# Feed-forward parts of a two-block transformer kernel: the first modulation pair leaves the weight ring for idle context columns

## The chip, the cores and the metric

The kernel runs on one core of one Trainium2 chip. The time is that of the device, in microseconds, from a launch with one program; three runs of the kernel before took 2731.29, 2735.66 and 2738.76 us. Five engines work side by side and wait for each other by semaphores: TensorE (PE in the profile, its weight loads PEld), VectorE (DVE), ScalarE (ACT), GpSimd (POOL) and SyncE (SP), which here only issues the DMA transfers.

## The reference, cut to what matters

Two blocks of different design are computed one after the other, all in float32, for 512 tokens of width 1024 and a context of 256 tokens.

```python
def first_block(x, ...):
    for layer in range(2):
        h = rmsnorm(x, norm_mix_g[layer])
        if layer == 0:                       # Fourier heads and convolution heads
            y = concat(fnet_heads(p[..., :512], ...), conformer_conv_heads(...)) @ w_out_ab
        else:                                # windowed means
            y = pool_mixer(h, pool_map, pool_scale)
        x = x + y
        h = rmsnorm(x, norm_ffn_g[layer])
        x = x + (silu(h @ w_gate[layer]) * (h @ w_up[layer])) @ w_down[layer]
    return rmsnorm(x, final_g)

def second_block(x, c, ctx, c_ctx, ...):
    for i in range(2):
        mod_x = silu(c) @ w_ada[i] + b_ada[i]          # six modulation vectors
        mod_c = silu(c_ctx) @ w_ada[i] + b_ada[i]
        ...                                            # attention over x and ctx (layer 0: window, 1: differential)
        x = layer_norm(alpha * x + g1 * ax, ln1_g[i], ln1_b[i])
        x = layer_norm(alpha * x + g2 * sqrelu_mlp(x * (1 + sc2) + sh2, ...), ln2_g[i], ln2_b[i])
        ...                                            # layer 0 only: the same for ctx
```

The modulation vectors depend on `c` alone, so the kernel computes those of layer f of the second block inside feed-forward part f of the first one: the weights `w_ada` are cut into pairs of blocks, and pair after pair is worked off beside the products of gate, up and down.

## The kernel before, in words

**Data.** Activations lie with the features on the partitions: `X`, `Ahi`, `Alo` are [128, 8, 768], eight tiles of features by 512 token columns and 256 context columns. A float32 product is made of three products of high and low parts (weight high x activation high, weight high x activation low, weight low x activation high), so every weight and every activation is split in two. In the whole first block only the token columns of `Ahi` and `Alo` are written or read; the context columns are first used by the norm n5 ahead of the attention.

**The weight stream.** All large weights are one list of blocks of 1 MB, `stream`, laid out by the host in the order of use. Block b goes to slot b % 3 of a ring (`RING = 3`, tiles `raw`, `whi`, `wlo`), in two halves. SP waits until PE has used the same half of block b - 3 (`freed`, by the counter `w_used`) and issues the load (L452). POOL splits each half: L526 writes `whi`, L528 writes `wlo` (semaphore `w_split`). Modulation blocks are not split: PE multiplies them from `raw` (`ada`, L868), or DVE sums them up (L1966, L1970). `SPLITS[b]` counts the splits ahead of block b, and `is_ada` says which blocks have none.

**Order on PE.** `columns` (L685) multiplies one block, or two in turns, tile k by tile k: for each k first gate's share, then up's (L675 by way of `product`). It waits for the split of the first half at k = 0 and of the second at k = 4, and, where a norm goes before, for the k-th tile of `Alo` (semaphore `ready`).

**A feed-forward part** (`swiglu`, one on each engine). Its 57 blocks in the ring begin with modulation pair 0 (two blocks), gate 0, up 0; then eleven steps follow, each with gate and up of the next step, a modulation pair and down of this step. PE first multiplies pair 0 (L868), then gate 0 and up 0 in turns. For the first part these are blocks 10 and 11 (pair), 12 (gate), 13 (up); in the second 68 to 71. So up 0 takes the slot of the pair's first block and its load waits for PE to have used that. Block 9, the last of the output projection, doesn't use the ring; it is loaded to the arena once the four Fourier heads are done.

**Later parts and the order on POOL.** POOL's work is one hand-written list: `split_run(first, end)` splits blocks, as a loop over whole rounds of the ring where there are two or more, and between these runs stand other jobs. One is `norm_residual` (L627 to L640): X times the norm's scale for eight tiles (L636; L634 for l2), then gain and bias for eight tiles (L639). It follows the layernorms l1, l2 and l3, waits for DVE's copy of the scale (`kept`; L1813, L1811), and makes the residual into which DVE adds an MLP's results. The places where the list is cut are given by `ring_end(b)` (L563), the next multiple of 3 at or above b:

```python
split_run(ring_end(B_WOA), ring_end(B_ML0 + 2))     # L643
norm_residual("l1", 1, X_CTX)
split_run(ring_end(B_ML0 + 2), ring_end(B_QKV + 2))
norm_residual("l2", 2, X_ONLY)
...
split_run(B_WOB, ring_end(B_ML1 + 2))               # L663
norm_residual("l3", 3, X_ONLY)
```

The block numbers before: pooling 67, keys and values 125, queries 127, window attention's output 131, first MLP (`B_ML0`) 135, differential attention's weights (`B_QKV`; query, key, value for each of four steps) 167, its output 179, second MLP (`B_ML1`) 183, 215 blocks in all.

**An MLP** (`mlp`): PE does up(0), then for each step up(i + 1) and down(i). Block +0 is up 0, +1 is up 1, +2 is down 0, +3 is up 2. A down product is eight tiles m; tile m waits until DVE has added the tile `slots` places earlier to X (`dfree`), with two slots where the context goes along (first MLP) and four without it (second). DVE's first addition (L2224) waits for the whole residual, `dve.wait_ge(l1_res or l3_res, 8)` at L2233.

**Differential attention**: PE does the query products, the key products (`key_products`), waits for both halves of the value block's split (L1217), does two tiles of value products (L1210) and then the first scores (L1233).

## Time and profile before

| | us |
|---|---|
| runs | 2731.29, 2735.66, 2738.76 (median 2735.66) |
| the profiled execution | 2737.59 |
| its span, first to last instruction | 2735.3 |
| PE busy | 2595.5 (95%) |
| DVE busy | 1478.3 (54%) |
| POOL busy | 1357.7 (50%) |
| ACT busy | 649.8 (24%) |
| mean granted TensorE clock | 0.978 |

PE is busy nearly all the time. Busy shares say little about a single wait, though: for that one reads a stretch of the timeline, in which each row has the start, the time, the engine, the line and the form of an instruction, and in brackets how long the engine sat idle before it and who released it. "PE ... [6.20 <-POOL wlo L528]" means that PE waited 6.20 us for POOL's write of `wlo`. The granted clock is a share of full speed, 1.00 for 2.4 GHz and 0.50 for 1.2 GHz. Where several equal instructions are merged, the row has their number (x8) and the time of all.

### The profile page before, as it was taken

Reading aid. Unit: us, or ns where it says so; the run is one execution under the profiler, and the core shown is the slowest. Engines: PE = TensorE matmul, PEld = TensorE weight load, DVE = VectorE, ACT = ScalarE, POOL = GpSimd, SP = SyncE. Lnnn points to the kernel's source line nnn. Section 1 sums busy time; section 2 is a strip of 40 time slices with the busy share of each in tenths; the row PEclk is TensorE's granted clock in tenths of the full one; section 3 lists DMA queues with packets and bytes.
Section 4 is the critical chain, followed back from the end, with each engine's and each line's share of the span. In section 5 each row is a group of like instructions: output and inputs, shape, how many; then the busy total and the mean of one; then the engine's idle time right before and its main releaser. Section 6 shows DMA issues by size and latency. Waiting matters only on the chain.

```text
span 2735.3 us, 39085 instructions
## 1 busy us (share of the span) xinstructions
PE 2595.5 (95%) x14176; PEld 2101.6 (77%) x14176; DVE 1478.3 (54%) x2473; ACT 649.8 (24%) x1220; POOL 1357.7 (50%) x880
## 2 busy tenths in 40 slices
PE   7989999999999989889989999999899999899997
PEld 6668777777777768656768888888688887688886
DVE  6955666456666645455454333333676665454445
ACT  2220000031000013477231111111265552211112
POOL 6374566645555663233536444444252515776661
PEclk9999999999999999899999999999999999999998
DMA  5124444434444441100111111221111011232321
GB/s 189 54 78 139 151 154 149 151 118 146 151 153 154 153 133 62 32 1 1 39 39 62 62 61 61 66 65 61 39 47 46 31 47 48 73 96 92 97 94 54
DMA packets 67388, 235.73 MB, mean 86 GB/s; under 512 B 8144, under 2 KB 9552, under 8 KB 67152
## 3 DMA queue, kind: packets, MB, share of 16 engines
q1 hardware_dynamic: 65792, 233.64, 26.5%
q8 instruction: 63, 1.03, 0.2%
q10 hardware_dynamic: 1488, 0.69, 0.1%
q14 instruction: 45, 0.37, 0.0%
HBM read 232.21 MB, written 2.10 MB: 86 GB/s over the span
## 4 chain that ended last, share of the span: by engine, by line
PE 87%; DVE 7%; ACT 2%; issue 2%; POOL 1%; DMA 1%; SPq 0%; DVEq 0%; ACTq 0%; POOLq 0%
PE ps L675 70%; PE ps L1210 2%; PE ps L1233 2%; PE ps L830 2%; PE ps L1098 2%; PE ps L1172 2%; PE ps L1084 1%; PE ps L794 1%; DVE X L1796 1%; PE ps L1164 1%; DVE Alo L1785 1%; DVE tmp L1778 1%; DMA raw<-in_stream 1%; PE ps L1059 1%; PE ps L718 1%
## 5 line engine op out<-in xcount | busy, mean ns | idle before, releaser
L526 POOL TENSOR_SCALAR whi<-raw 128x1024 fp32r<-128x1024 f32 x332 | 372.8, 1123 | 1019.5 <-DMA raw<-in_stream 1019.2
L528 POOL TENSOR_TENSOR wlo<-raw,whi 128x1024 fp32r<-128x1024 f32 x332 | 804.2, 2422 | 27.7
L675 PE MATMUL ps<-Ahi,whi 128*128 128x512 f32 (+1 forms) x2128 | 728.2, 373 | 40.4 <-DVE Alo L1785 18.8
L675 PE MATMUL ps<-Alo,whi 128*128 128x512 f32 (+1 forms) x2128 | 721.8, 370 | 0.0
L675 PE MATMUL ps<-Ahi,wlo 128*128 128x512 f32 (+1 forms) x2128 | 719.2, 369 | 0.0
L2224 DVE SCALAR_TENSOR_TENSOR X<-ps,modT,X 128x512 f32<-128x512 f32 (+1 forms) x384 | 242.4, 659 | 476.7 <-PE ps L675 476.5
L675 PEld LDWEIGHTS ps<-Ahi,whi 128*128 128x128 f32 x2128 | 375.7, 190 | 120.6 <-DVE Alo L1785 18.9
L675 PEld LDWEIGHTS ps<-Ahi,wlo 128*128 128x128 f32 x2128 | 376.2, 190 | 69.6
L675 PEld LDWEIGHTS ps<-Alo,whi 128*128 128x128 f32 x2128 | 376.7, 191 | 66.7 <-issue 0.7
L675 PE MATMUL ps<-hhi,whi 128*128 128x512 f32 x1120 | 373.6, 370 | 2.1 <-DVE X L2224 1.1
L675 PE MATMUL ps<-hhi,wlo 128*128 128x512 f32 x1120 | 373.4, 370 | 0.0
L675 PE MATMUL ps<-hlo,whi 128*128 128x512 f32 x1120 | 370.4, 368 | 0.0
L675 PEld LDWEIGHTS ps<-hhi,whi 128*128 128x128 f32 x1120 | 192.6, 188 | 45.5 <-issue 4.4
L675 PEld LDWEIGHTS ps<-hlo,whi 128*128 128x128 f32 x1120 | 192.3, 188 | 38.9
L675 PEld LDWEIGHTS ps<-hhi,wlo 128*128 128x128 f32 x1120 | 192.4, 188 | 38.5
L1326 ACT ACTIVATE hhi<-tmp 128x512 fp32r<-128x512 f32 (+1 forms) x108 | 73.7, 695 | 606.3 <-DVE tmp L2210 445.5
L1970 DVE SCALAR_TENSOR_TENSOR ps<-raw,arena,ps 128x256 f32<-128x256 f32 x432 | 174.0, 480 | 41.7 <-DMA raw<-in_stream 41.7
L1994 DVE TENSOR_TENSOR X<-ps,X 128x512 f32<-128x512 f32 x176 | 121.7, 692 | 137.3 <-PE ps L675 136.9
L1326 ACT ACTIVATE arena<-ps 128x256 f32<-128x256 f32 (+5 forms) x194 | 101.6, 543 | 245.4 <-PE ps L889 67.3
L625 POOL TENSOR_SCALAR tmp<-tmp,sm 128x256 f32<-128x256 f32 (+2 forms) x96 | 63.3, 662 | 148.1 <-DVE sm L2179 148.0
L1476 ACT ACTIVATE tmp<-ps 128x512 f32<-128x512 f32 x44 | 26.3, 598 | 425.0 <-PE ps L675 424.0
L1623 ACT ACTIVATE tmp<-ps 128x512 f32<-128x512 f32 x96 | 47.1, 525 | 293.1 <-PE ps L675 290.8
(300 smaller groups left out, 2851.0 us busy)
## 6 DMA issues: line engine op xcount, KB each, us to landing
raw<-in_stream SPq DMA_DIRECT2D x428, 512.0 KB, 3.8
X<-in_xT SPq DMA_DIRECT2D x2, 1024.0 KB, 6.6
arena<-in_dft SPq DMA_DIRECT2D x1, 2048.0 KB, 17.1
out_xT<-X SPq DMA_DIRECT2D x2, 1024.0 KB, 4.3
X<-in_ctxT SPq DMA_DIRECT2D x1, 1024.0 KB, 19.4
w<-in_stream SPq DMA_DIRECT2D x2, 512.0 KB, 4.3
vec<-in_vec SPq DMA_DIRECT2D x1, 364.5 KB, 7.7
arena<-in_fmap SPq DMA_DIRECT2D x1, 256.0 KB, 12.6
```

The costliest lines, as they stand in the source:

```text
L526: pool.tensor_scalar(whi[:, s, part], raw[:, s, part], 1.0, 1.0, ALU.mult, ALU.mult).then_inc(sem("w_hi"), 1)
L528: pool.tensor_tensor(wlo[:, s, part], raw[:, s, part], whi[:, s, part], ALU.subtract).then_inc(sem("w_split"), 1)
L625: pool.tensor_scalar(prob, prob, sm[:, u % 8, 2:3], 1.0, ALU.mult, ALU.mult).then_inc(sem("pA"), 1)
L675: mm = pe.matmul(dst[c], w[:, b % RING, off:off + P], rhs(k, part, c0, n), start=(k == 0 and w is whi and part == 0), stop=(k == kn - 1 an ...
L830: mm = pe.matmul(ps[:, WOUT_BANK[j], :], w[:, at:at + P], a[:, k, 0:T], start=(k == 0 and w is hi and a is Ahi), stop=(k == KT - 1 and w i ...
L1098: mm = pe.matmul(ps[DH * h:DH * h + DH, 6, 0:2 * P], vA[:, ks[t], DH * g:DH * g + DH], heads[:, h], start=(t == 0), stop=(t == len(ks) - 1 ...
L1172: mm = pe.matmul(ps[:, 6, :], vB[:, t, hh * P:(hh + 1) * P], aT[:, t, :], start=(t == 0), stop=(t == NTT - 1))
L1210: mm = pe.matmul(ps[:, 6 + t % 2, 0:256], a[:, k, t * P:(t + 1) * P], w[:, (B_QKV + 2) % RING, k * 256:(k + 1) * 256], start=(k == 0 and a ...
L1326: return act.activation(dst, src, ACT.Copy, scale=scale)
L1970: mm = dve.scalar_tensor_tensor(out=to, in0=row, scalar=c, in1=acc, op0=ALU.mult, op1=ALU.add)
L1994: dve.tensor_tensor(X[:, m, 0:T], ps[:, 4 + m % 2, :], X[:, m, 0:T], ALU.add).then_inc(sem(f"{name}_dfree"), 1)
L2224: mm = dve.scalar_tensor_tensor(out=X[:, m, c0:c0 + n], in0=ps[:, 4 + len(cols) * (m % (4 // len(cols))) + c, 0:n], scalar=mod(l, 5, m, c) ...
```

## The change

The first modulation pair of each feed-forward part is taken out of the ring. Its two blocks go straight to the context columns of `Ahi` and of `Alo`, which lie unused in the first block (`first_pair`, `load_first_pair`); PE multiplies them from there (`ada_first`), at the same place as before. The stream in memory stays as it was; the ring skips two blocks of it for each part, so that a part has 55 blocks in the ring, the ring's block numbers after the second part are lower by 4, and loads add 2 or 4 to find a block in memory. Gate 0 and up 0 are now the first blocks of a part in the ring (10 and 11; 66 and 67). Their halves are split in turns: gate's first, up's first, gate's second, up's second (`split_pair`); the same is done for the first two blocks of the input projection and of the window attention's output projection, and PE's waits in `columns` follow that order. The list of POOL is otherwise written as before, with the new block numbers in it: pooling 65, keys and values 121, queries 123, window attention's output 127, `B_ML0` 131, `B_QKV` 163, its output 175, `B_ML1` 179, and 211 blocks in the ring.

The diff, without the hunks that only change block offsets in DVE's and ACT's steps:

```diff
--- before.py
+++ after.py
@@ -111,7 +111,7 @@
 
 B_WIN = 0
 B_WOUT = B_WIN + 6
-FF_BLOCKS = 5 * FF_IT + 2
+FF_BLOCKS = 5 * FF_IT
 B_FF = [B_WOUT + 4, B_WOUT + 4 + FF_BLOCKS + 1]
 B_POOL = B_FF[0] + FF_BLOCKS
 B_KV = B_FF[1] + FF_BLOCKS
@@ -122,7 +122,8 @@
 B_QKV = B_ML0 + ML_BLOCKS
 B_WOB = B_QKV + 12
 B_ML1 = B_WOB + 4
-N_BLOCKS = B_ML1 + ML_BLOCKS
+RING_BLOCKS = B_ML1 + ML_BLOCKS
+N_BLOCKS = RING_BLOCKS + 4
 B_ML = [B_ML0, B_ML1]
 
 
@@ -131,17 +132,17 @@
     for first in B_FF:
         at = b - first
         if 0 <= at < FF_BLOCKS:
-            if at < 4:
-                return at < 2
+            if at < 2:
+                return False
             if at >= FF_BLOCKS - 3:
                 return at < FF_BLOCKS - 1
-            return (at - 4) % 5 in (1, 3)
+            return (at - 2) % 5 in (1, 3)
     return False
 
 
 
 SPLITS = [0]
-for _b in range(N_BLOCKS):
+for _b in range(RING_BLOCKS):
     SPLITS.append(SPLITS[-1] + (0 if is_ada(_b) else 2))
 FF_SPLITS = 18
 ADA_GROUP = 32
@@ -247,6 +248,10 @@
         Ahi = sb("Ahi", [P, KT, TT], F32R)
         Ahi_at = nc.sbuf_base - 4 * KT * TT
         Alo = sb("Alo", [P, KT, TT], F32R)
+        Alo_at = nc.sbuf_base - 4 * KT * TT
+
+        first_pair = [nc.alloc_sbuf_tensor_at(f"pair{e}", [P, KT, TT], F32, offset=at)[:, :, T:TT]
+                      for e, at in enumerate((Ahi_at, Alo_at))]
 
         whi = sb("whi", [P, RING, BLK], F32R)
         raw = sb("raw", [P, RING, BLK])
@@ -469,6 +474,14 @@
                 for half in range(2):
                     sp.wait_ge(*when("w_used", 2 * (b - RING) + half + 1))
                     load(b, b % RING, half)
+            def load_first_pair(f):
+
+                if f:
+                    sp.wait_ge(*when("pair_used", 2))
+                for e in range(2):
+                    sp.dma_start(first_pair[e], ins["stream"][B_FF[f] + 2 * f + e].rearrange("p (k c) -> p k c", k=KT)).then_inc(sem(f"pair{e}"), 16)
+
+            load_first_pair(0)
             sp.wait_ge(*when("y_done", HEADS_A))
             for half in range(2):
                 part = slice(half * HALF, (half + 1) * HALF)
@@ -477,37 +490,42 @@
             def freed(b, half, rounds=0):
                 sp.wait_ge(*when("w_used", 2 * RING * rounds + (2 * (b - RING) + half + 1)))
 
-            def load_run(first, end):
+            def load_run(first, end, skipped):
+
                 for b in range(first, end):
                     for half in range(2):
                         freed(b, half)
-                        load(b, b % RING, half)
+                        load(b + skipped, b % RING, half)
 
             def load_swiglu(f):
                 B0 = B_FF[f]
+                S = B0 + 2 * f + 4
+                load_run(B0, B0 + 2, 2 * f + 2)
                 with sp.Fori(0, FF_IT // 3) as p:
-                    for b in range(B0 + 4, B0 + 19):
-                        at = (b - B0 - 4) // 5 * 5 + B0 + 4 + FF_ORDER[(b - B0 - 4) % 5]
+                    for n in range(15):
+                        at = n // 5 * 5 + S + FF_ORDER[n % 5]
                         for half in range(2):
-                            freed(b, half, 5 * p)
-                            load(15 * p + at, b % RING, half)
-                for b in range(B0 + 49, B0 + 54):
+                            freed(B0 + 2 + n, half, 5 * p)
+                            load(15 * p + at, (B0 + 2 + n) % RING, half)
+                for n in range(45, 53):
+                    at = S + (45 + FF_ORDER[n - 45] if n < 50 else n)
                     for half in range(2):
-                        freed(b, half)
-                        load(B0 + 49 + FF_ORDER[b - B0 - 49], b % RING, half)
-
-            load_run(last + 1, B_FF[0] + 4)
+                        freed(B0 + 2 + n, half)
+                        load(at, (B0 + 2 + n) % RING, half)
+
+            assert last + 1 == B_FF[0]
             load_swiglu(0)
-            load_run(B_FF[0] + 54, B_FF[1] + 4)
+            load_run(B_POOL, B_POOL + 1, 2)
+            load_first_pair(1)
             load_swiglu(1)
-            first, rounds = -(-(B_FF[1] + 54) // RING), N_BLOCKS // RING
-            load_run(B_FF[1] + 54, first * RING)
+            first, rounds = -(-B_KV // RING), RING_BLOCKS // RING
+            load_run(B_KV, first * RING, 4)
             with sp.Fori(first, rounds) as i:
                 for s in range(RING):
                     for half in range(2):
                         freed(s, half, i)
-                        load(RING * i + s, s, half)
-            load_run(rounds * RING, N_BLOCKS)
+                        load(RING * i + (s + 4), s, half)
+            load_run(rounds * RING, RING_BLOCKS, 4)
 
 
             for h in range(2):
@@ -531,6 +549,12 @@
 
                 for half in range(2):
                     split(b % RING, half, 16 * rounds + (16 * (b // RING) + 16), more + (SPLITS[b] + half + 1))
+
+            def split_pair(b):
+
+                for half in range(2):
+                    for n in range(2):
+                        split((b + n) % RING, half, 16 * ((b + n) // RING) + 16, SPLITS[b] + 2 * half + n + 1)
 
             def split_run(first, end):
 
@@ -549,15 +573,14 @@
 
             def split_swiglu(f):
                 B0 = B_FF[f]
-                for b in (B0 + 2, B0 + 3):
-                    split_block(b)
+                split_pair(B0)
                 with pool.Fori(0, FF_IT // 3) as p:
                     for s in range(3):
                         for b in (0, 2, 4):
-                            split_block(B0 + 4 + 5 * s + b, FF_SPLITS * p, 5 * p)
+                            split_block(B0 + 2 + 5 * s + b, FF_SPLITS * p, 5 * p)
                 for i in range(FF_IT // 3 * 3, FF_IT - 1):
                     for b in (0, 2, 4):
-                        split_block(B0 + 4 + 5 * i + b)
+                        split_block(B0 + 2 + 5 * i + b)
                 split_block(B0 + FF_BLOCKS - 1)
 
             def ring_end(b):
@@ -606,7 +629,8 @@
                     pool.tensor_tensor(ending[:, side, :, e0:e0 + EDGE], own[:, :, e0:e0 + EDGE], edge[:, :, side, :],
                                        ALU.add).then_inc(sem("bands"), 1)
 
-            split_run(0, B_WOUT + 3)
+            split_pair(B_WIN)
+            split_run(2, B_WOUT + 3)
             for half in range(2):
                 b = B_WOUT + 3
                 part = slice(half * HALF, (half + 1) * HALF)
@@ -618,7 +642,8 @@
             split_swiglu(0)
             split_block(B_POOL)
             split_swiglu(1)
-            split_run(B_KV, ring_end(B_WOA))
+            split_run(B_KV, B_WOA)
+            split_pair(B_WOA)
             for u in range(N_UNITS):
                 pool.wait_ge(*when("denA", u + 1))
                 prob = probA[u % 4][:, 1:1 + len(keys(UNITS[u][2])) * P]
@@ -640,7 +665,7 @@
                                        ALU.add).then_inc(sem(f"{name}_res"), 1)
 
 
-            split_run(ring_end(B_WOA), ring_end(B_ML0 + 2))
+            split_run(B_WOA + 2, ring_end(B_ML0 + 2))
             norm_residual("l1", 1, X_CTX)
             split_run(ring_end(B_ML0 + 2), ring_end(B_QKV + 2))
             norm_residual("l2", 2, X_ONLY)
@@ -662,7 +687,7 @@
                     split_run(B_QKV + 11, B_WOB)
             split_run(B_WOB, ring_end(B_ML1 + 2))
             norm_residual("l3", 3, X_ONLY)
-            split_run(ring_end(B_ML1 + 2), N_BLOCKS)
+            split_run(ring_end(B_ML1 + 2), RING_BLOCKS)
 
 
         @block.tensor
@@ -691,7 +716,7 @@
                         pe.wait_ge(*when(ready, k + 1))
                     for n, (ws, at) in enumerate(blocks):
                         if k % 4 == 0:
-                            pe.wait_ge(*when("w_split", ws + (k // 4 + 1)))
+                            pe.wait_ge(*when("w_split", ws + (k // 4 + 1 if len(blocks) == 1 else k // 2 - n + 1)))
                         for j in range(2):
                             mm = product(dsts[2 * n + j], cols, at, k * 256 + j * P, a_rhs, k, KT)
                             if j == 0 and k == KT - 1:
@@ -871,6 +896,16 @@
                                        skip_group_check=True)
                     mm.then_inc(sem("w_used"), 1)
 
+            def ada_first(f, e):
+
+                pe.wait_ge(*when(f"pair{e}", 16 * f + 16))
+                for k in range(KT):
+                    g = k % 4
+                    mm = pe.matmul(ps[ADA_GROUP * g:ADA_GROUP * (g + 1), 6 + e, 0:256],
+                                   csil[:, k, 2 * (ADA_SHARED - 1):2 * (ADA_SHARED - 1) + ADA_GROUP], first_pair[e][:, k, :],
+                                   start=(k < 4), stop=(k >= 4), skip_group_check=True)
+                mm.then_inc(sem("pair_used"), 1)
+
             def ada_select(name, copies):
 
                 pe.wait_ge(*when(f"{name}_arow", copies))
@@ -928,13 +963,13 @@
                             ada_columns(name, copies)
 
                 for e in range(2):
-                    ada(B0 + e, e, 0, 1)
-                columns(f"{name}_up", [(SPLITS[b], b) for b in (B0 + 2, B0 + 3)], X_ONLY, banks[0:4], ready)
+                    ada_first(f, e)
+                columns(f"{name}_up", [(SPLITS[b], b) for b in (B0, B0 + 1)], X_ONLY, banks[0:4], ready)
                 ada_select(name, 2)
 
                 with pe.Fori(0, FF_IT // 3) as p:
                     for s in range(3):
-                        i, at = 3 * p + s, B0 + 4 + 5 * s
+                        i, at = 3 * p + s, B0 + 2 + 5 * s
                         for part in range(2):
                             up(i + 1, at, FF_SPLITS * p, part)
                             if s == 0 and part == 0:
...
@@ -1459,16 +1494,19 @@
             def swiglu(f, name):
                 B0 = B_FF[f]
 
-                def rows(b_a, gap):
+                def rows(b_a):
                     for e in range(2):
-                        act.wait_ge(*block_used(b_a + gap * e))
+                        if b_a is None:
+                            act.wait_ge(*when("pair_used", 2 * f + e + 1))
+                        else:
+                            act.wait_ge(*block_used(b_a + e))
                         copy(arow[:, e, :], ps[:, 6 + e, 0:256]).then_inc(sem(f"{name}_arow"), 1)
 
                 def step(i, b, slot, first, shared_rows=False):
 
                     for j in range(2):
                         if j:
-                            act.wait_ge(*block_used(b + 2 if first else b))
+                            act.wait_ge(*block_used(b))
                         else:
                             act.wait_ge(*when(f"{name}_up", 2 * i + 1))
                         if not first:
...
```

## Rows read from the trace of the kernel before

**Rows 1.** The page: the span and the busiest engine, and the chain by engine.

```profile
span 2735.3 us, 39085 instructions
...
PE 87%; DVE 7%; ACT 2%; issue 2%; POOL 1%; DMA 1%; SPq 0%; DVEq 0%; ACTq 0%; POOLq 0%
```

**Rows 2.** The page, DMA issues: count, KB each, median us from issue to landing.

```profile
raw<-in_stream SPq DMA_DIRECT2D x428, 512.0 KB, 3.8
```

**Rows 3.** Timeline of PE, 187 to 202: start, us, form, [idle before <-releaser].

```profile
190.01 0.50 PE L675 MATMUL ps<-Ahi,whi 128*128 128x512 f32 x1 [0.46 <-DVE Alo L1754]
...
197.87 0.80 PE L675 MATMUL ps<-Ahi,whi 128*128 128x512 f32 x1 [6.20 <-POOL wlo L528]
```

**Rows 4.** Timeline of POOL, 185 to 198.

```profile
185.90 1.05 POOL L526 TENSOR_SCALAR whi<-raw 128x1024 fp32r<-128x1024 f32 x1 [18.12 <-DMA raw<-in_stream]
...
195.16 2.66 POOL L528 TENSOR_TENSOR wlo<-raw,whi 128x1024 fp32r<-128x1024 f32 x1
```

**Rows 5.** Stretches of PE: us, busy (matmuls), granted clock, DMA share, GB/s.

```profile
197.80:201.90 4.10, 4.03 (x10) 0.50 0.02 5
...
205.00:215.00 10.00, 10.00 (x46) 1.00 0.17 52
...
622.90:628.60 5.70, 5.70 (x13) 0.50 0.34 104
```

**Rows 6.** Timeline of PE, 616 to 624.

```profile
622.90 0.79 PE L675 MATMUL ps<-Ahi,whi 128*128 128x512 f32 x1 [4.93 <-POOL wlo L528]
```

**Rows 7.** Timeline of DVE, 617 to 624.

```profile
617.99 0.68 DVE L1754 TENSOR_TENSOR Alo<-tmp,Ahi 128x512 fp32r<-128x512 f32 x1
...
620.56 0.73 DVE L1763 SCALAR_TENSOR_TENSOR tmp<-X,vec,ps 128x512 f32<-128x512 f32 x1
...
621.22 2.17 DVE L1754 TENSOR_TENSOR Alo<-tmp,Ahi 128x512 fp32r<-128x512 f32 x1
```

**Rows 8.** Timeline of PE, 19 to 29.

```profile
23.22 0.79 PE L675 MATMUL ps<-Ahi,whi 128*128 128x512 f32 x1 [0.74 <-POOL wlo L528]
```

**Rows 9.** Stretch, all engines: busy (x) of each, then granted clock, DMA share, GB/s.

```profile
105.00:130.00 25.00, 25.00 (x74) 10.93 (x72) 24.92 (x39) 6.76 (x10) 0.00 (x0) 1.00 0.00 1
```

**Rows 10.** Timeline of PE, 1428 to 1456.

```profile
1430.59 0.52 PE L675 MATMUL ps<-Ahi,wlo 128*128 128x512 f32 x2
...
1453.14 0.51 PE L675 MATMUL ps<-hhi,whi 128*128 128x512 f32 x2
```

**Rows 11.** Timeline of POOL, 1400 to 1450.

```profile
1424.80 17.34 POOL L636 TENSOR_TENSOR X<-X,rstd 128x768 f32<-128x768 f32 x8 [27.88 <-DVE rstd L1813]
1442.14 7.77 POOL L639 TENSOR_SCALAR X<-X,rg,rb 128x768 f32<-128x768 f32 x8
```

**Rows 12.** Line L636 of POOL, 1424 to 1432: min/median/max ns.

```profile
L636 POOL TENSOR_TENSOR X<-X,rstd x5: 1825/1837/2575, 1424.8 to 1432.0; 128x768 f32<-128x768 f32 x5
```

**Rows 13.** Timeline of DVE, 1445 to 1453.

```profile
1451.34 1.14 DVE L2224 SCALAR_TENSOR_TENSOR X<-ps,modT,X 128x512 f32<-128x512 f32 x2 [10.92 <-PE ps L675]
```

**Rows 14.** Timeline of PE, 2367 to 2386.

```profile
2368.75 0.49 PE L675 MATMUL ps<-Ahi,whi 128*128 128x512 f32 x1 [0.77 <-ACT tmp L1623]
...
2385.37 0.39 PE L675 MATMUL ps<-hhi,whi 128*128 128x512 f32 x1
```

**Rows 15.** Timeline of POOL, 2355 to 2381.

```profile
2363.27 11.83 POOL L636 TENSOR_TENSOR X<-X,rstd 128x512 f32<-128x512 f32 x8 [15.88 <-DVE rstd L1813]
2375.09 6.05 POOL L639 TENSOR_SCALAR X<-X,rg,rb 128x512 f32<-128x512 f32 x8
```

**Rows 16.** Timeline of DVE, 1986 to 1989.

```profile
1987.82 0.68 DVE L1811 COPY X<-ps 128x512 f32<-128x512 f32 x1
```

**Rows 17.** Timeline of POOL, 1985 to 2018.

```profile
1999.74 11.02 POOL L634 TENSOR_TENSOR X<-X 128x512 f32<-128x512 f32 x8
```

**Rows 18.** Timeline of PE, 2002 to 2014.

```profile
2004.61 0.28 PE L1210 MATMUL ps<-whi,Ahi 128*128 128x256 f32 x1
...
2013.01 1.30 PE L1233 MATMUL ps<-k,q 128*128 128x384 f32 x6 [2.48 <-DVE rstd_r L2284]
```

More of the change, by code:

```diff
@@ L944, in swiglu @@
                 i = FF_IT - 2
-                at = B0 + 4 + 5 * i
+                at = B0 + 2 + 5 * i
                 for part in range(2):
@@ L952, in swiglu @@
                 i = FF_IT - 1
-                b = B0 + 4 + 5 * i
+                b = B0 + 2 + 5 * i
                 for e in range(2):
@@ L1482, in step @@
                         copy(hhi[:, slot, j, 0:T], tmp[:, j, 0:T]).then_inc(sem(f"{name}_hi"), 1)
-                rows(B0, 1)
+                rows(None)
                 step(0, B0, 0, True)
@@ L1487, in swiglu @@
                     for s in range(3):
-                        step(3 * p + s + 1, 15 * p + (B0 + 4 + 5 * s), (s + 1) % 3, False, s == ADA_SHARED - 1)
-                step(FF_IT - 1, B0 + 4 + 5 * (FF_IT - 2), (FF_IT - 1) % 3, False)
-                rows(B0 + 4 + 5 * (FF_IT - 1), 1)
+                        step(3 * p + s + 1, 15 * p + (B0 + 2 + 5 * s), (s + 1) % 3, False, s == ADA_SHARED - 1)
+                step(FF_IT - 1, B0 + 2 + 5 * (FF_IT - 2), (FF_IT - 1) % 3, False)
+                rows(B0 + 2 + 5 * (FF_IT - 1))
             rms("n2", "wout_evac", 0)
@@ L2009, in swiglu @@
                 for j in range(2):
-                    hidden(0, B0 + 3, j, True)
+                    hidden(0, B0 + 1, j, True)
                 mods(0, 0, 1)
@@ L2016, in swiglu @@
                         for e in range(2):
-                            ada_sums(p, 3 * p + s, e, B0 + 5 + 5 * s + 2 * e, s or e)
+                            ada_sums(p, 3 * p + s, e, B0 + 3 + 5 * s + 2 * e, s or e)
                         if s == ADA_SHARED - 1:
                             dve.wait_ge(*when(f"{name}_acc", ADA_SUMS * ADA_SHARED * (p + 1)))
-                        step(3 * p + s, 15 * p + (B0 + 4 + 5 * s), (s + 1) % 3, p if s == ADA_SHARED - 1 else None)
-                step(FF_IT - 2, B0 + 4 + 5 * (FF_IT - 2), (FF_IT - 1) % 3, last=True)
+                        step(3 * p + s, 15 * p + (B0 + 2 + 5 * s), (s + 1) % 3, p if s == ADA_SHARED - 1 else None)
+                step(FF_IT - 2, B0 + 2 + 5 * (FF_IT - 2), (FF_IT - 1) % 3, last=True)
                 mods(4, 10, 2)
```

## The prediction

> **What bounds the kernel now.** I read the page's chain first: TensorE (PE) carries 87% of the path that ends last, and the span is 2735.3 us [rows 1]. So an edit is worth what it adds to or takes from PE's idle time, plus what that idle time costs in clock. Second, I looked in the timelines of PE for the gaps at the places the diff touches, and third, in those of POOL and DVE, for what stands behind each gap. POOL is the engine that splits each half block of weights into a high and a low part, and it runs a list in a fixed order; what the change does to that order matters as much as the waits it means to remove.
>
> **Part 1, the starts of the feed-forward parts: a gain.** At the first one PE does gate's share of k = 0 from 190.01 and then waits 6.20 us for the low part of up's first half [rows 3]. POOL begins the four halves of gate and up only at 185.90, when gate's first half lands behind the two modulation blocks, and finishes the third, up's first, at 195.16 + 2.66 = 197.8 [rows 4]. After the wait PE runs 4.1 us at a granted clock of 0.50, the lower level of 1.2 GHz, with some ten matmuls where the later stretch at 1.00 has 46 in 10 us [rows 5]; half of that time is lost: 2.05. At the second part the wait is 4.93 us [rows 6], followed by 5.7 us at 0.50 [rows 5], 2.85 lost. There up's block could not even be loaded before PE had used the modulation block in its slot. Together 6.2 + 2.05 + 4.93 + 2.85 = 16.0 us.
>
> With the pair outside the ring, gate and up of the first part wait for the two blocks of the output projection that the pair waited for, so gate is released two blocks, some 24 matmuls or 5.4 us, earlier: POOL starts by 180.5. At 1.50 + 2.70 a half under contention (the spacing that makes 185.90 to 197.8 out of three halves is 4.0), up's first half, now second in line, is done by 188.9, before PE's first product at 190.01 [rows 3]; gate's second half is done by 193.1 and up's by 197.3, and PE needs them after 48 matmuls, at about 200.5. What is late next is DVE's low part of the activations, whose steps take 0.73 + 0.68 = 1.4 us alone and 0.73 + 2.17 = 2.9 us where a split is in the way, every second one at most [rows 7], against 12 matmuls, 2.7 us, of PE work for each; I cost that at nothing. At the second part both blocks are released when the first part ends, some 30 us ahead: no wait is left.
>
> The pair's own loads (2 x 1 MB, in pieces of 1 KB) cost SP two issues. The first two stand ahead of SP's wait for the Fourier heads, in a stretch in which the DMA engines are idle, its later part at 0.00 [rows 9]; the second two stand behind the pooling block's load and ahead of gate's. The trace has no load of that shape: at nothing, since over 30 us cover it, or, if the pieces took three times the 3.8 us of a half block [rows 2] each half, 23 us more ahead of gate's load, still covered. PE's sixteen pair matmuls stay the same in number and place.
>
> Splitting earlier puts POOL beside DVE's closing additions and norm. DVE's subtraction of two SBUF operands takes 0.68 us alone and 2.17 us once POOL splits; its product that reads PSUM stays at 0.73 us in the same stretch [rows 7]. The subtractions were beside splits before as well, and what newly lies beside them (additions from PSUM, the scaled products) is of the second kind, so this is nothing. The Trainium skill, "SBUF — State Buffer", section "Who interferes with whom", says that a DVE instruction with two SBUF inputs contends with a GpSimd instruction that reads SBUF, and one with at most one does not: the trace agrees. Were every DVE instruction slowed, two on the chain to the first product would cost 3 us, and the sum would be 3 us higher.
>
> **Part 2, the first projection's halves in turns: a small gain.** PE waits 0.74 us for its second block's first half [rows 8]; in turns this half is second in POOL's list instead of third. PE is at the low clock around it, and a row without the pause may let the clock rise sooner: 0.7 to 2.5 us, 1.0 taken. The same turns at the attention's output projection: its splits are ready there already, nothing.
>
> **Part 3, the ring is four blocks shorter: losses that the diff doesn't show.** Every later block has a number lower by 4, and 4 is not a multiple of 3. `ring_end(b)` rounds up to a multiple of 3, and POOL's list is cut there: it splits up to `ring_end(...)`, then does `norm_residual`, then splits on.
>
> *l1.* Before, B_ML0 is 135 and the cut 138: POOL splits the MLP's blocks +0, +1, +2 and then does the residual. After, B_ML0 is 131 and the cut 135: +3 goes ahead of the residual as well, and its slot is that of +0, so its second half can be loaded only when PE has finished the MLP's first product, at 1431.1 [rows 10]. Plus 3.8 us of landing [rows 2] is 1434.9; plus 3.5 to 4.2 for the split, 1438.8. Before, the residual starts at 1424.80 and ends at 1449.9 [rows 11]. Its products take 1.84 us beside nothing [rows 12], so now 1438.8 + 8 x 1.84 + 7.77 = 1461.3. DVE may add down's results to X only after it; its first addition, 1.14 us for both column groups [rows 13], ends at 1462.4 instead of 1452.5. Down has two slots, so PE's third tile waits for it: it begins at 1453.14 now [rows 10], 9.3 us later then. PE idles this long, and comes back at the low clock [rows 5]: 2.4 more (the mean of 2.05 and 2.85). **11.7 us.**
>
> *l3.* B_ML1 goes from 183 to 179, the cut from +3 to +4: the same. The first product ends at 2368.75 - 0.77 = 2368.0 [rows 14]; landing 2371.8; split 2375.7. The residual took 11.83 + 6.05 [rows 15]; alone, by the width, 8 x 1.84 x 2/3 = 9.8, so 10.5 taken: 2392.2; one addition, 1.14 for 768 columns [rows 13] and so some 0.8 for 512: 2393.0. Here four slots stand, and PE's fifth tile begins at 2385.37 [rows 14]: 7.6 later, with the clock **10.0 us**.
>
> *l2.* B_QKV goes from 167 to 163, the cut from +4 back to +2: the residual comes ahead of the split of the value weights (+2). It can start when DVE's copy ends, 1988.5 [rows 16], and takes 11.02 + 6.05 (the second figure is that of the other residual of this width) [rows 15, 17]: 2005.6. Two halves at 3.5 to 4.2: 2013.0. PE begins the value products at 2004.61 today [rows 18], and they last until 2013.01 - 2.48 = 2010.5, 5.9 us: to 2018.9 then, and the scores follow at 2018.9 instead of 2013.01. 5.9, and with the clock **8.3 us**.
>
> **The sum.** Gains 16.0 + 1.0 = 17.0, losses 11.7 + 10.0 + 8.3 = 30.0: 13.0 us slower, 2748.3 against the profiled span. The profiled execution took 2737.6 with what lies around its span, the median of the runs is 2735.7, so I add the 13.0 to the median: 2748.7.
>
> **The rivals.**
> *Hidden residuals, faster.* The three residuals are later, but PE isn't held: DVE would find other work, or the blocks land sooner. Then only the gains are left, 2735.7 - 17.0 = 2718.7. It decides the other way from the point at which l1's residual ends before about 1451, ten us earlier than worked out. DVE's list has the addition next, and nothing in the trace lets it pass; the rows speak against it.
> *No clock cost.* The pauses of 6 to 9 us don't bring the clock down, or PE's work behind them has slack. For it: DVE has room to catch up. Against: both pauses before [rows 5]. Losses 22.8, so +5.8: 2741.5.
> *The gate still waits.* The change doesn't do what it says: gate or up land late, say because the pair's small pieces hold the queue, and the 16.0 stay. 2764.7. Against: the queue is empty there for tens of us.
>
> **How the numbers follow.** Forecast 0.68, hidden residuals 0.07, no clock cost 0.19, still waiting 0.06. About 8 us (0.3%) is what a measurement of this kernel can tell from no change. Slower 0.68 + 0.06 = 0.74, same 0.19, faster 0.07. The forecast's own ends: gains 15 to 19, losses 28 to 33 (splits at 4.2, the clock at 2.05 or 2.85), so 2744.7 to 2753.7; reaching down over the second rival and leaving 2 us for rounding of both, and up for a fourth pause that I haven't seen, 2739 to 2757.
>
> **What would show it.** Right: no PE wait on `wlo` at the two starts and 1.00 of clock there; PE pauses of about 9, 6 to 8 and 8 us in the first down of both MLPs and ahead of the first value product, with POOL's residual at some 1461 (less the gains before it) as the cause; POOL splitting two more halves between `rstd`'s copy and l1's residual. Wrong: no such pauses, or one at the starts still. An own load of the pair that lands after PE asks for it would show as a wait on DMA at the pair's matmuls.

## The result and the profile after

Seven runs of the changed kernel took 2745.68 to 2752.09 us, median 2747.95; seven of the kernel before, at the same time, 2731.29 to 2741.75, median 2736.72. The ratio is 1.0037 with a 95% interval of 1.0027 to 1.0048: slower, by 7.4 to 13.1 us. The forecast was 13.0 us slower, 2748.7; it lies near the upper end of this interval.

The page of the changed kernel: the span, PE's busy time, and the chain by engine.

```profile
span 2745.1 us, 39030 instructions
...
PE 2593.7 (94%) x14176; PEld 2104.3 (77%) x14176; DVE 1460.5 (53%) x2473; ACT 649.3 (24%) x1220; POOL 1347.6 (49%) x880
...
PE 86%; DVE 7%; POOL 2%; ACT 2%; issue 2%; DMA 1%; DVEq 0%; SPq 0%; POOLq 0%; ACTq 0%
```

PE is busy for as long as before (2593.7 against 2595.5 us) and the span is 9.8 us longer, so the difference is in PE's idle time: 151.4 us, before 139.8. POOL's share of the chain has gone from 1% to 2% [rows 1]: it now sits on the path for longer. PE's waits, in total, times, longest, show where; of the list these two are new:

```profile
PE ps L700 <- DVE X L2262: 17.7, 3, 9.0
...
PE ps L1245 <- POOL wlo L546: 8.7, 1, 8.7
```

Before, PE waited for this line of DVE once, for 1.1 us, and for POOL's `wlo` three times, 11.9 us in all, at the two starts and in the first projection [rows 3, 6, 8]. Those three waits are gone, and three others are there.

**By stage.** Equal events cut both spans into the same six stretches. The marks are instructions of PE: the spread of the norm's scale ahead of the first feed-forward part (184.94 before, 182.06 after), the same ahead of the second (611.90, 603.92), the first product of the first MLP (1411.25, 1392.52), the first query product (1973.81, 1966.55), the first product of the second MLP (2354.71, 2354.76) and the end. The same table, in us, for all profiled executions of this study:

| | to 1st part | 1st part, pooling | 2nd part, window attention | 1st MLP | differential attention | 2nd MLP |
|---|---|---|---|---|---|---|
| before | 184.9 | 427.0 | 799.4 | 562.6 | 380.9 | 380.6 |
| after | 182.1 | 421.9 | 788.6 | 574.0 | 388.2 | 390.3 |
| `cuts_all` | 182.1 | 422.0 | 789.8 | 563.8 | 382.9 | 381.6 |
| `before_late` | 185.1 | 426.9 | 795.8 | 574.1 | 387.1 | 390.4 |
| `cut_l1` | 181.4 | 420.6 | 790.8 | 563.8 | 388.8 | 390.2 |
| `cut_l2` | 183.0 | 422.0 | 793.9 | 575.4 | 380.7 | 391.5 |
| `cut_l3` | 182.2 | 421.9 | 787.7 | 574.7 | 388.2 | 380.5 |
| `no_turns` | 181.8 | 417.8 | 788.7 | 562.8 | 378.1 | 380.6 |
| `before_turns` | 184.6 | 426.0 | 797.2 | 563.4 | 383.0 | 381.6 |
| `cuts_v` | 181.8 | 420.5 | 790.3 | 562.5 | 377.5 | 380.6 |
| `win_turns` | 181.6 | 427.2 | 795.9 | 562.6 | 378.4 | 380.6 |
| `hold` | 183.1 | 418.5 | 790.5 | 563.0 | 379.6 | 380.7 |

From before to after: -2.9, -5.1, -10.8, +11.5, +7.3, +9.8, together +9.8. Both attention stages vary by 5 to 6 us between rows in which that stage has the same order of work (787.7 to 793.9, and 378.1 to 383.0), the MLP stages by about 1, so the attention stages are read over all rows. These rows are one execution each, of different kernels. Much of this spread is PE's clock. `cut_l2` (793.9) has a granted clock of 0.91 over a stretch in which `cut_l3` (787.7) is at 1.00 (us, busy (matmuls), granted clock, DMA share, GB/s; `cut_l2` first):

```profile
1146.00:1200.00 54.00, 44.73 (x294) 0.91 0.00 1
```

```profile
1145.00:1199.00 54.00, 43.55 (x315) 1.00 0.01 1
```

At 0.91 some 9% of 54 us, about 5 us, are lost (an estimate: PE is busy throughout its stretches at 0.50 there). Why the clock differs isn't shown.

**The loss in the first MLP.** POOL's timeline of the changed kernel:

```profile
1374.35 1.04 POOL L544 TENSOR_SCALAR whi<-raw 128x1024 fp32r<-128x1024 f32 x1 [6.32 <-DMA raw<-in_stream]
...
1406.67 1.05 POOL L544 TENSOR_SCALAR whi<-raw 128x1024 fp32r<-128x1024 f32 x1 [28.83 <-DMA raw<-in_stream]
...
1415.10 1.04 POOL L544 TENSOR_SCALAR whi<-raw 128x1024 fp32r<-128x1024 f32 x1 [4.91 <-DMA raw<-in_stream]
...
1418.58 14.45 POOL L661 TENSOR_TENSOR X<-X,rstd 128x768 f32<-128x768 f32 x8
...
1433.03 7.71 POOL L664 TENSOR_SCALAR X<-X,rg,rb 128x768 f32<-128x768 f32 x8
```

The last block that it can split early is done at 1375.47 + 2.38 = 1377.9. Then it waits 28.83 us for a half block whose slot PE must free first, splits it, waits 4.91 us for the other half, and only then, at 1418.58, begins the residual. In the kernel before the residual began right after DVE's copy, without a split in between [rows 11]. It ends at 1440.7; DVE's addition follows at 1441.08, and PE's third tile of down starts here:

```profile
1442.28 1.01 PE L700 MATMUL ps<-hhi,whi 128*128 128x512 f32 x2 [8.97 <-DVE X L2262]
```

The forecast had a pause of 9.3; it is 8.97. In the second MLP the half block, the end of the residual, and PE's fifth tile:

```profile
2371.71 1.45 POOL L544 TENSOR_SCALAR whi<-raw 128x1024 fp32r<-128x1024 f32 x1 [2.01 <-DMA raw<-in_stream]
...
2385.61 6.01 POOL L664 TENSOR_SCALAR X<-X,rg,rb 128x512 f32<-128x512 f32 x8
```

```profile
2392.76 0.79 PE L700 MATMUL ps<-hhi,whi 128*128 128x512 f32 x1 [7.67 <-DVE X L2262]
```

The forecast had 7.6; it is 7.67. And at l2, the residual ahead of the value block's split (which ends 2006.0), and PE's first value product:

```profile
1981.31 10.97 POOL L659 TENSOR_TENSOR X<-X 128x512 f32<-128x512 f32 x8 [46.12 <-DVE X L1849]
...
1998.70 1.04 POOL L544 TENSOR_SCALAR whi<-raw 128x1024 fp32r<-128x1024 f32 x1
...
2003.65 2.35 POOL L546 TENSOR_TENSOR wlo<-raw,whi 128x1024 fp32r<-128x1024 f32 x1
```

```profile
2006.22 0.57 PE L1245 MATMUL ps<-whi,Ahi 128*128 128x256 f32 x1 [8.73 <-POOL wlo L546]
```

All three pauses are followed by the lower clock. Stretches of PE, in the same columns:

```profile
1442.30:1446.00 3.70, 3.70 (x11) 0.50 0.00 0
2006.20:2010.00 3.80, 3.78 (x17) 0.50 0.00 0
2392.70:2396.00 3.30, 3.24 (x8) 0.54 0.00 0
```

The first two are at 0.50 throughout, 3.7 and 3.8 us long, so 1.9 us each are lost at the least; in the third the clock is back at 1.00 near its end.

**The gain at the first feed-forward part.** The wait on `wlo` has gone, but PE's wait on DVE ahead of the first product has grown to 2.38 us from 0.46 [rows 3], and the seven matmuls behind it run at the lower clock:

```profile
187.45 0.80 PE L700 MATMUL ps<-Ahi,whi 128*128 128x512 f32 x1 [2.38 <-DVE Alo L1792]
...
187.40:190.60 3.20, 3.15 (x7) 0.50 0.03 5
```

POOL starts at 176.46, 9.4 us earlier than before [rows 4], and its third low part at 184.50:

```profile
176.46 1.05 POOL L544 TENSOR_SCALAR whi<-raw 128x1024 fp32r<-128x1024 f32 x1 [11.87 <-DMA raw<-in_stream]
...
184.50 2.35 POOL L546 TENSOR_TENSOR wlo<-raw,whi 128x1024 fp32r<-128x1024 f32 x1
```

DVE's first subtraction of two SBUF operands starts 0.2 us after that and takes 2.70 us (below it the same instruction of the kernel before, 1.45 us):

```profile
184.70 2.70 DVE L1792 TENSOR_TENSOR Alo<-tmp,Ahi 128x512 fp32r<-128x512 f32 x1
```

```profile
188.50 1.45 DVE L1754 TENSOR_TENSOR Alo<-tmp,Ahi 128x512 fp32r<-128x512 f32 x1
```

The low part of POOL beside which the latter ran:

```profile
187.04 2.37 POOL L528 TENSOR_TENSOR wlo<-raw,whi 128x1024 fp32r<-128x1024 f32 x1
```

Both subtractions end at the same distance behind the low part of POOL beside which they ran: that of the changed kernel ends at 186.85 and the subtraction at 187.40, those of the kernel before at 189.41 and 189.95. So the subtraction is held until POOL's instruction is over, and the earlier it begins beside it, the longer it takes.

The pair's four loads took 9.3 us each to land, in the median:

```profile
pair<-in_stream SPq DMA_DIRECT2D x4, 1024.0 KB, 9.3
```

PE has no wait on them.

### The profile page after: what moved, and what is told of

It is laid out like the page before. It is cut to its first block, busy times and chain, and to the rows that moved or that the text cites. A ratio compares the mean times of both kernels' runs of the same rounds, so it can differ in the third digit from the quotient of the medians.

```text
span 2745.1 us, 39030 instructions
## 1 busy us (share of the span) xinstructions
PE 2593.7 (94%) x14176; PEld 2104.3 (77%) x14176; DVE 1460.5 (53%) x2473; ACT 649.3 (24%) x1220; POOL 1347.6 (49%) x880
## 4 chain that ended last, share of the span: by engine, by line
PE 86%; DVE 7%; POOL 2%; ACT 2%; issue 2%; DMA 1%; DVEq 0%; SPq 0%; POOLq 0%; ACTq 0%
PE ps L700 68%; PE ps L1245 2%; PE ps L1268 2%; PE ps L855 2%; PE ps L1207 2%; PE ps L1133 2%; PE ps L1119 1%; PE ps L819 1%; POOL X L661 1%; PE ps L743 1%; PE ps L733 1%; PE ps L1199 1%; DVE X L1834 1%; DVE Alo L1823 1%; DVE tmp L1816 1%
## 5 line engine op out<-in xcount | busy, mean ns | idle before, releaser
L700 PEld LDWEIGHTS ps<-hhi,whi 128*128 128x128 f32 x1120 | 193.7, 189 | 62.8 <-DVE X L2262 18.8
```

The source lines that it names most:

```text
L700: mm = pe.matmul(dst[c], w[:, b % RING, off:off + P], rhs(k, part, c0, n), start=(k == 0 and w is whi and part == 0), stop=(k == kn - 1 an ...
```

## Experiments

Each names its edit against the kernel that it starts from.

**`cuts_all`: POOL's list cut at the old places.** Against the changed kernel:

```diff
-split_run(B_WOA + 2, ring_end(B_ML0 + 2))
+split_run(B_WOA + 2, B_ML0 + 3)
 norm_residual("l1", 1, X_CTX)
-split_run(ring_end(B_ML0 + 2), ring_end(B_QKV + 2))
+split_run(B_ML0 + 3, B_QKV + 4)
 norm_residual("l2", 2, X_ONLY)
...
-split_run(B_WOB, ring_end(B_ML1 + 2))
+split_run(B_WOB, B_ML1 + 3)
 norm_residual("l3", 3, X_ONLY)
```

> The changed kernel, with POOL's list cut at the same blocks as in the kernel before: +3 of the first MLP, +4 of the differential attention's weights, +3 of the second MLP, instead of +4, +2, +4. Theory (the three losses all come from where the residuals stand in POOL's list): the spans between equal events of the two traces put them at 12.7, 8.0 and 10.2 us, so 30.9 go and 2747.95 becomes 2717, some 20 us under the kernel before; no PE wait on DVE's first addition in either MLP and none on wlo ahead of the value products. Rival A (the later parts are slow for another reason that goes with the new block numbers, other slots or other DMA timing): 2748 stays. Rival B (one wait takes the place of another, the gain of one cut is given back in the next): 2725 to 2740.

Measured: 2724.79 us in the median (2722.74 to 2725.76), ratio to the kernel before 0.9949 (0.9935 to 0.9963). The three waits are gone, and their stages are back at 563.8, 382.9 and 381.6. Ahead of the scores stands again the wait of before [rows 18]:

```profile
1997.07 1.32 PE L1268 MATMUL ps<-k,q 128*128 128x384 f32 x3 [2.62 <-DVE rstd_r L2322]
```

The cuts are the cause of the loss: from 1.0037 to 0.9949 is 24 us. That is less than the 30.9 expected from two single traces, and the time lies at the edge of rival B's range (2725), 8 us above the expected 2717. Rival B's mechanism isn't there: PE's waits show none that took over. By the table the three stages went down by 10.2, 5.3 and 8.7 us, and those ahead of them up by 1.3. Two of the 8 us are in the expectation, whose 12.7, 8.0 and 10.2 are 2.3 more than the table's 11.5, 7.3 and 9.8. The rest is that these stages stand 1.2, 2.0 and 1.0 us above the kernel before in this one execution; in `cuts_v` and `hold` both MLP stages are back at its values to 0.4.

**`before_late`: the losses alone.** Against the kernel before:

```diff
-split_run(ring_end(B_WOA), ring_end(B_ML0 + 2))
+split_run(ring_end(B_WOA), B_ML0 + 4)
...
-split_run(ring_end(B_ML0 + 2), ring_end(B_QKV + 2))
+split_run(B_ML0 + 4, B_QKV + 2)
...
-split_run(B_WOB, ring_end(B_ML1 + 2))
+split_run(B_WOB, B_ML1 + 4)
```

> The kernel before with nothing changed but the three cuts of POOL's list, put at +4, +2 and +4 blocks as the changed kernel has them. Theory: the losses alone, without the gains: 2736.7 + 30.9 = 2768, with PE waits of some 9, 8 and 8 us at the two MLPs' first down and ahead of the first value products. Rival (the losses need the new slots or the pair's place): 2737.

Measured: 2762.84 us, ratio 1.0092 (1.0076 to 1.0107), 25 us slower, where 30.9 were expected. The waits on DVE's addition, and the one on `wlo` (PE's instruction), have the size of those in the changed kernel:

```profile
PE ps L675 <- DVE X L2224: 17.6, 3, 9.0
...
2021.53 0.58 PE L1210 MATMUL ps<-whi,Ahi 128*128 128x256 f32 x1 [8.76 <-POOL wlo L528]
```

So the losses need neither the new slots nor the pair's new place, only POOL's order.

**`cut_l1`, `cut_l2`, `cut_l3`: one cut each.** Against the changed kernel, the one line of each in `cuts_all`.

> The changed kernel with the first cut alone put back to +3. Theory: 12.7 us of loss go, 2735.3. Rival (the losses hang on each other, so that a later wait takes over what an earlier one frees): 2740 to 2748.

Measured: 2739.74 us, ratio 1.0008 (0.9996 to 1.0021), by the ratios 7.9 us less than the changed kernel, where 12.7 were expected. The time is at the edge of the rival's range (2740). Its stage went from 574.0 to 563.8, the other two stayed at 388.8 and 390.2: nothing was handed on.

> The changed kernel with the second cut alone put back to +4, so that the value weights are split before l2's residual. Theory: 8.0 us go, 2740. Rival: DVE's key subtraction, which before ended the wait at this place (2.48 us), takes over, and POOL's later residual contends with it: 4 us at most, 2744.

Measured: 2743.77 us, ratio 1.0027 (1.0012 to 1.0042). Its stage went from 388.2 to 380.7 and the wait ahead of the values is gone, yet by the ratios the whole is only 2.7 us less than the changed kernel, and the two intervals overlap. The execution that was profiled was 5 us long in a stage without an edit (793.9, with the lower clock shown above). By its stage the theory holds; its time is that of the rival (2744), so the time doesn't settle it.

> The changed kernel with the third cut alone put back to +3. Theory: 10.2 us go, 2737.8. Rival (DVE has slack behind the pause, so that part of it is caught up anyway): 5 us or less, 2743 to 2748.

Measured: 2740.04 us, ratio 1.0008 (0.9998 to 1.0018), by the ratios 7.9 us less. Its stage went from 390.3 to 380.5, so nothing of the pause had been caught up.

**`no_turns`: the order of the halves in the feed-forward parts undone.** Against `cuts_all`:

```diff
-split_pair(B0)
+for b in (B0, B0 + 1):
+    split_block(b)
```

with PE's waits to match.

> As cuts_all, but in the feed-forward parts POOL splits gate's two halves and then up's two, not in turns; PE's waits follow. Theory from the changed trace: the third half is done at 186.85 and the first product starts at 187.45, so the order is worth nothing at the first part, and nothing at the second either (all four halves done long before): the same as cuts_all, 2717. Rival (my prediction's step: a half takes 4.2 us there and POOL starts at 180.5): the third half is done 3 us after PE's first product, then the pause costs 3 and a low clock 2: 2722.

Measured: 2721.69 us, ratio 0.9943 (0.9928 to 0.9959), the same as `cuts_all` within the intervals. The order is worth little there, but not quite nothing. With PE's first product 2.4 us earlier than in `cuts_all`, PE does wait for the low part of up's first half, which is third in POOL's list again:

```profile
187.39 0.50 PE L701 MATMUL ps<-Ahi,whi 128*128 128x512 f32 x1 [0.57 <-POOL wlo L546]
```

The trace has more: this execution's first subtraction began at 184.41, POOL's low part at 184.57, and DVE's took its plain time while POOL's took 2.77 instead of 2.35. First DVE, then POOL:

```profile
184.41 0.69 DVE L1793 TENSOR_TENSOR Alo<-tmp,Ahi 128x512 fp32r<-128x512 f32 x1
```

```profile
184.57 2.77 POOL L546 TENSOR_TENSOR wlo<-raw,whi 128x1024 fp32r<-128x1024 f32 x1
```

In `cuts_all` POOL's began at 184.57 and DVE's at 184.77, and DVE's took 2.70. So in one and the same place a shift of 0.4 us, which changes who comes first, decides over 2 us on PE's path. The first part's stage is 417.8 instead of 420.5 to 422.0. Not all of that is this wait: the granted clock is 1.00 throughout this stage, while all other kernels with the pair outside the ring have a stretch of some 3.5 us at the lower clock near 590, in the pooling layer, worth 1.7 us (that of the changed kernel first, then `no_turns`):

```profile
590.10:593.60 3.50, 3.50 (x18) 0.51 0.23 77
```

```profile
587.00:594.00 7.00, 6.92 (x58) 1.00 0.16 56
```

**`before_turns`: the turns alone, the pair still in the ring.** Against the kernel before, `split_pair(B0 + 2)` in place of gate's and up's blocks one after the other.

> The kernel before with the halves of gate and up in turns in the feed-forward parts, and the modulation pair still in the ring. Theory (the place of the pair in the ring causes the wait, the turns hardly help): at the first part up's first half lands some 3.8 us after PE has used the modulation block's first half at 187.6, and its split ends near 195.7 instead of 197.8, 2 us gained; at the second part it was loaded late anyway, nothing: 2734.7. Rival (the order of the halves is what made PE wait): most of 16 us, 2721.

Measured: 2736.20 us, ratio 0.9991 (0.9981 to 1.0001). PE still waits at both starts:

```profile
196.01 0.79 PE L680 MATMUL ps<-Ahi,whi 128*128 128x512 f32 x1 [4.51 <-POOL wlo L528]
...
621.28 0.79 PE L680 MATMUL ps<-Ahi,whi 128*128 128x512 f32 x1 [4.46 <-POOL wlo L528]
```

4.51 instead of 6.20, and 4.46 instead of 4.93; the wait ahead of the first part's first product is 0.86, before 0.46. The place in the ring is the cause of the waits, not the order of the halves.

**`cuts_v`: the second cut at +3.** Against `cuts_all`, `B_QKV + 3` in place of `B_QKV + 4`.

> As cuts_all, but the second cut at +3 instead of +4: value weights split, then l2's residual, then the next step's query weights. Theory (only the value weights are urgent there): the same as cuts_all within 2 us, 2717. Rival (the residual's early start contends with DVE's rotations and subtractions, on which the scores wait): 2 to 5 us slower.

Measured: 2720.45 us, ratio 0.9938 (0.9923 to 0.9952), the same as `cuts_all` within the intervals, and no slower. Only the value weights must be ahead of the residual.

**`hold`: POOL stands back for the norm.** Against `cuts_v`:

```diff
 for half in range(2):
+    if half and hold:
+        pool.wait_ge(*when(hold, 1))      # hold = "n2_out" in the first part
     for n in range(2):
```

with `hold = "n2_out"` in the first part and none in the second.

> As cuts_v, and at the first feed-forward part POOL, after the first halves of gate and up, waits for the first tile of the norm's low part before it splits the second halves. Theory (the pause of 2.4 us ahead of the first product is DVE's first subtraction of two SBUF operands, held up by POOL's split that began 0.2 us earlier, 2.70 us instead of 0.68, and the low clock behind the pause costs 1.5 more): the subtraction takes 0.7, no PE pause over 0.6 us and a clock of 1.00; from the norm's spread to the spread of the next norm 417 us instead of 420.5 to 422; 3.5 us less than cuts_v's 2720.45 where the rest holds still, 2717. Rival (the wait is of the norm itself, or the second halves now come late at k = 4): the pause stays or moves ten us on, 2720 to 2725.

Measured: 2717.43 us (2715.14 to 2719.04), ratio 0.9917 (0.9903 to 0.9930). DVE's subtraction takes 0.69 us, POOL starts its third half behind it, and over the ten us that follow, the PE clock is 1.00 (all engines' busy times, then clock, DMA share, GB/s):

```profile
185.78 0.69 DVE L1794 TENSOR_TENSOR Alo<-tmp,Ahi 128x512 fp32r<-128x512 f32 x1
```

```profile
182.50 2.35 POOL L546 TENSOR_TENSOR wlo<-raw,whi 128x1024 fp32r<-128x1024 f32 x1
186.69 1.05 POOL L544 TENSOR_SCALAR whi<-raw 128x1024 fp32r<-128x1024 f32 x1 [1.84 <-DVE Alo L1794]
```

```profile
185.00:195.00 10.00, 9.63 (x61) 7.46 (x54) 9.96 (x11) 3.80 (x6) 8.14 (x5) 1.00 0.01 2
```

The stage is 418.5, not 417, and no wait has come at k = 4. The theory holds for the wait. For the clock behind it `cuts_v` itself says no: its pause was 2.45 us, and all that followed ran at the higher clock.

```profile
187.28 0.50 PE L700 MATMUL ps<-Ahi,whi 128*128 128x512 f32 x1 [2.45 <-DVE Alo L1792]
```

```profile
187.28:190.60 3.32, 3.32 (x15) 1.00 0.02 5
```

In `cut_l1` the pause was 2.54 us, with the higher clock behind it too. So the edit gives back 2.0 us against an execution like that of `cuts_v` (420.5) and 3.5 against one like that of `cuts_all` (422.0), which had the lower clock. The median is 3 us below that of `cuts_v`, with intervals that overlap, and was taken on another chip, so of the edit by itself the stage says more. The version as a whole is faster than both kernels, by 0.83% than the one before.

**`win_turns`: the turns in the first projection alone.** Against the kernel before, `split_pair(B_WIN)` and `split_run(2, B_WOUT + 3)` in place of `split_run(0, B_WOUT + 3)`.

> The kernel before with turns in the first projection alone. Theory (the 2.9 us by which the changed kernel is ahead at the norm of the first feed-forward part come from this edit: the pause of 0.74 and its clock): that norm's spread at 182.0 instead of 184.94, all later stages as before, 2735. Rival (they come from the pair's absence or from drift): 184.9.

Measured: 2735.29 us, ratio 0.9988 (0.9975 to 1.0000). The first stage is 181.6 instead of 184.9. PE has no pause after its first products and reaches the higher clock at 22.4, where the kernel before had a pause ahead of 23.22 [rows 8] and the lower clock until 28.0:

```profile
19.26 0.80 PE L682 MATMUL ps<-Ahi,whi 128*128 128x512 f32 x1 [4.10 <-DVE Alo L1761]
...
22.36 0.40 PE L682 MATMUL ps<-Alo,whi 128*128 128x512 f32 x1
```

## Why the prediction was right

The time lies 0.75 us from the forecast, and most of the steps were right on their own; three gains were off and cancelled out in part. That the number is as close as this is luck: by the ratio the loss is 10.1 us, not 13.0, and the runs of one kernel differ among themselves by 6 to 10 us.

- *Losses.* l1: 11.7 forecast, 11.5 by its stage; l3: 10.0 and 9.8; l2: 8.3 and 7.3. Each term of the sums can be seen: the landing (4.0 us from the end of the first product at 1411.15 to POOL's start at 1415.10, against 3.8), a split of 3.5, eight products of 1.81. Over all rows of the table, too, the stages with a loss are 11.5, 7 and 10 us longer than those without. `cuts_all` and `before_late`, from opposite sides, make the whole 24 and 25 us by the ratios against 30 forecast and 28.6 by the stages. With their intervals (some 19 to 29, and 21 to 29 us) both still allow 28.6; whether the whole is a few us less isn't settled.
- *The second part's start.* 7.8 forecast; over all executions the stage is 797.0 with the old wait (four of them) and 790.0 without (eight), 7.0.
- *The first part's start.* 8.2 forecast, 5.1 measured. The failed step is "this is nothing" for splitting beside DVE's norm. The subtraction on which PE's first product hangs lay beside a low part before as well, but began 1.46 us into it and took 1.45 us; now it begins 0.2 us into it and takes 2.70. PE's pause there is 1.9 us longer than the old one, and behind it seven matmuls ran at the lower clock in this execution, 1.5 us. Together that is a little more than the 3.1 that are missing. Two other stretches of 3.5 us at the lower clock about balance: one from 184.9 in the kernel before, which is gone, and the one from 590.1 in the changed kernel. `hold` brought back 2.0 us against `cuts_v` and 3.4 against the changed kernel's 421.9, the part between being the clock. The Trainium skill, "SBUF — State Buffer", section "Who interferes with whom", says that issue order decides who blocks: the traces of `cuts_all` and `no_turns` agree (2.70 us for DVE's subtraction in one, 0.69 in the other), and this sentence of the page was the one to weigh.
- *The step that made turns necessary.* POOL was to start by 180.5 and take 4.2 us a half; it started at 176.46, 2.9 of this because the whole first stage was shorter, and took 3.45, so the third half was done at 186.85, before PE's first product. The wait was gone as forecast, but the turns in the feed-forward parts carry little: without them PE waits 0.57 us once DVE isn't late (`no_turns`).
- *The first projection.* 1.0 forecast in a range of 0.7 to 2.5; 2.9, with `win_turns` at 3.4 for the profiled execution. The term was mis-sized: after a pause of 0.74 us the lower clock lasted 4.8 us more, and without it the rise came 3.0 to 5.7 us after the first product (earliest in `cut_l1`, latest in `cut_l2` and `hold`). Over all rows the stage is 184.6 to 185.1 with the pause and 181.4 to 183.1 without.
- *Rivals.* Hidden residuals fell with the pauses of 8.97, 8.73 and 7.67 us; no clock cost fell with the 0.50 behind them; the gate that still waits fell with the first part's timeline.

Of the net, 2.9 + 5.1 + 10.8 = 18.8 us gained in the changed execution against 28.6 lost; the forecast had 17.0 and 30.0. With the second part's start at the 7.0 of all executions, the gains are 15.0 and the net is 13.6; of the 10.8 some 4 us are the spread of that stage.

## What to carry to other kernels

Where an in-order engine's list is cut by rounding a block number to the ring's length, taking blocks out of the stream moves other work across those cuts, far from the edit; list what stands on each side of every such cut before and after. What must not wait for a freed slot belongs ahead of any split whose slot isn't free yet. And where one engine is moved earlier beside another that feeds the critical one, look at which of their instructions slow each other and who begins first: one wait of POOL on DVE's first result took 2.0 us off the stage here, and more where the pause was followed by the lower clock.

## What the runs showed of the hardware

- DVE's subtraction of two SBUF operands takes 0.69 us, and 2.70 when POOL's subtraction began 0.2 us ahead of it; begun 0.16 us ahead of POOL's, it takes 0.69 and POOL's is the one that is longer (2.77 instead of 2.35). In the changed kernel, the kernel before, `cuts_all`, `cut_l3`, `before_turns` and `win_turns` the held subtraction began 0.2 to 1.5 us into POOL's and ended 0.54 or 0.55 us behind it each time.
- Behind a PE pause of 2.38 us seven matmuls ran at the lower clock; ahead of the pause PE had done 1.9 us of small matmuls. At the same place in the kernel before, the pause was 0.46 us and the six matmuls behind it ran at the higher clock. But the length of the pause alone doesn't decide: in `cuts_v` and `cut_l1` it was 2.45 and 2.54 us at this place, and everything behind it ran at the higher clock, while in `cut_l3` a pause of 2.12 us was followed by the lower one.
- 1 MB in pieces of 1 KB landed in 9.3 us in the median, two such loads one behind the other, where 512 KB in pieces of 4 KB took 3.8.
- Executions of kernels that are alike in a stage differ there by 5 to 6 us (787.7 to 793.9), and the granted clock shows most of it: 0.91 for 54 us of that stage in the long one, 1.00 for the same stretch in the short one. A difference of this size in one trace says nothing of an edit.
